# A hybrid decoder step: position bias as two more columns of the compression's products, and three reordered places

## The reference

```python
def nsa_compress(kv, w_ck1, w_ck2, w_cv1, w_cv2, pe_k, pe_v):     # CMP_STRIDE 16, CMP_BLK 32, CMP_HID 128
    ch = kv.reshape(B, n_chunks, 16, 2, NSA_KV_HEADS, HEAD_DIM)
    blocks = jnp.concatenate([ch[:, j:j + n_cmp] for j in range(2)], axis=2)
    def mlp(x, pe, w1, w2):
        x = (x + pe[None, None, :, None, :]).transpose(0, 3, 1, 2, 4).reshape(B, NSA_KV_HEADS, n_cmp, 32 * HEAD_DIM)
        return jax.nn.silu(x @ w1) @ w2
    kc = mlp(blocks[:, :, :, 0], pe_k, w_ck1, w_ck2)
    vc = mlp(blocks[:, :, :, 1], pe_v, w_cv1, w_cv2)

z = rmsnorm(x, g_attn_norm) @ w_in        # prompt 512 rows, samples 8 rows; q, k, v, compression k/v, gates
y = rmsnorm(x3, g_final)                  # x3: the residual after the MLP; y_prompt and y_sample
```

## Time and profile before

| what | us |
|---|---|
| launches: median of 3 (lowest, highest) | 1170.24 (1166.24, 1178.13) |
| the profiled execution's own time | 1176.75 |
| its span in the trace | 1174.9 |
| TensorE products busy | 1080.7 (92%) |
| VectorE, ScalarE, GpSimd busy | 620.0, 393.0, 61.7 |
| mean granted TensorE clock, as a share of full speed | 0.933 |

### The profile page before, as it was taken

One profiled execution on the slowest core, in us unless ns is written; L12 is line 12 of the kernel. 1 busy time (PEld: TensorE's weight loads), 2 busy tenths in 40 slices (PEclk: granted clock), 3 DMA queues, 4 the chain that ended last, 5 costly groups with the idle time before them and its releaser, 6 DMA issues.

```text
span 1174.9 us, 23099 instructions
## 1 busy us (share of the span) xinstructions
PE 1080.7 (92%) x8348; PEld 953.1 (81%) x8348; DVE 620.0 (53%) x1052; ACT 393.0 (33%) x729; POOL 61.7 (5%) x83
## 2 busy tenths in 40 slices
PE   5996999998999898889998988999999999998994
PEld 4995999887888886555555557999999999998994
DVE  4333663577778677676444446445543334553334
ACT  4220112333333334656445345322221112221223
POOL 1000001211111100000000000110000000000000
PEclk9997996798999987899999998999999999999998
DMA  8537229599999963165766671323333333333221
GB/s 301 171 115 150 79 87 238 155 262 242 256 263 274 254 209 125 62 202 183 238 195 206 207 226 37 90 72 89 89 108 90 89 90 89 90 89 90 85 78 73
DMA packets 180323, 177.61 MB, mean 151 GB/s; under 512 B 13127, under 2 KB 140868, under 8 KB 177892
## 3 DMA queue, kind: packets, MB, share of 16 engines
q1 hardware_dynamic: 178536, 169.72, 51.4%
q10 hardware_dynamic: 1724, 7.04, 1.8%
HBM read 170.83 MB, written 10.06 MB: 154 GB/s over the span
## 4 chain that ended last, share of the span: by engine, by line
PE 63%; SPq 18%; issue 6%; DVE 5%; DMA 4%; ACT 3%; ACTq 0%; DVEq 0%
PE bank L658 59%; SPq L572 4%; PE bank L662 4%; SPq L494 3%; SPq L536 2%; SPq L560 2%; SPq L539 2%; SPq L487 2%; DMA low_arena<-in_cache_nsa_slc_kv_dram 2%; DMA high_arena<-in_w_in_dram 1%; DMA page_ids<-in_page_table_dram 0%; DMA high_arena<-in_cache_sb_kv_dram 0%; SPq L578 0%; SPq L500 0%; DVE high_arena L2197 0%
## 5 line engine op out<-in xcount | busy, mean ns | idle before, releaser
L658 PE MATMUL bank<-high_arena 128*128 128x254 f32 (+8 forms) x1864 | 241.3, 345 | 17.0 <-DMA high_arena<-in_cache_sb_kv_dram 7.3
L658 PEld LDWEIGHTS bank<-high_arena 128*128 128x128 f32 (+5 forms) x1864 | 187.5, 153 | 53.8 <-issue 12.6
L2126 DVE TENSOR_TENSOR w_low<-high_arena,w_high 128x1024 fp32r<-128x1024 f32 x72 | 90.1, 1251 | 78.8 <-ACT w_high L1502 68.8
L662 PE MATMUL bank<-low_arena 128*128 128x128 f32 (+3 forms) x658 | 106.6, 307 | 23.4 <-DMA low_arena<-in_cache_nsa_slc_kv_dram 11.5
L1502 ACT ACTIVATE w_high<-high_arena 128x1024 fp32r<-128x1024 f32 x72 | 76.4, 1061 | 144.4 <-PE bank L658 144.4
L662 PEld LDWEIGHTS bank<-low_arena 128*128 128x128 f32 (+3 forms) x658 | 87.5, 163 | 33.6 <-DMA low_arena<-in_cache_nsa_slc_kv_dram 12.2
L658 PE MATMUL bank<-a_high,w_high 128*128 128x256 f32 (+1 forms) x512 | 103.6, 284 | 5.3 <-issue 2.9
L658 PE MATMUL bank<-h_high,w_high 128*128 128x256 f32 (+1 forms) x512 | 103.7, 284 | 1.8 <-DVE h_low L2153 1.8
L658 PE MATMUL bank<-h_high,w_low 128*128 128x256 f32 (+1 forms) x512 | 103.8, 284 | 0.0
L658 PE MATMUL bank<-h_low,w_high 128*128 128x256 f32 (+1 forms) x512 | 103.8, 284 | 0.0
L658 PE MATMUL bank<-a_low,w_high 128*128 128x256 f32 (+1 forms) x512 | 103.2, 283 | 0.0
(11 more groups left out here) (226 smaller groups left out, 1583.3 us busy)
## 6 DMA issues: line engine op xcount, KB each, us to landing
low_arena<-in_cache_sb_kv_dram SPq DMA_DIRECT2D x128, 256.0 KB, 5.3
high_arena<-in_cache_sb_kv_dram SPq DMA_DIRECT2D x128, 256.0 KB, 3.5
high_arena<-in_cache_nsa_cmp_kv_dram SPq DMA_DIRECT2D x128, 128.0 KB, 5.3
high_arena<-in_w_up_dram SPq DMA_DIRECT2D x32, 512.0 KB, 4.0
high_arena<-in_w_down_dram SPq DMA_DIRECT2D x32, 512.0 KB, 4.2
high_arena<-in_w_in_dram SPq DMA_DIRECT2D x10, 1136.0 KB, 5.6
low_arena<-in_cache_nsa_slc_kv_dram SPq DMA_DIRECT2D x128, 64.0 KB
high_arena<-in_cache_nsa_slc_kv_dram SPq DMA_DIRECT2D x128, 64.0 KB, 2.4
```

The source lines that it names most:

```text
L658: return T.matmul(out, lhsT=l, rhs=r, start=start, stop=stop, **k)
L662: return T.transpose(out, in_, ident[0:n, 0:n])
L2126: V.tensor_tensor(w_lo_r[u], w_raw[u], w_hi[u], ALU.subtract).then_inc(sem(f"w_lo{u}"), 1)
```

## The change

Four edits. (1) Position bias: DVE writes the embedding as two further columns (32 and 33) of `xT`, so that the prompt's products of 66 instead of 62 columns form the bias in the last column of each head; the 32 one-column products and the common wait go. DVE copies the bias out of the bank for keys and for values apart (`bias(kv)`), and ACT waits for it before the sigmoid's first step. (2) SP loads block 6 before the first 8 pages of sample 0, block 7 before the other 8, then blocks 8 and 9. (3) At the start PE takes the samples' and six blocks of tile 0 before `vrow`; DVE scales tile 1 before it copies `vcol`; ACT makes two of the copies of `h_high` before the second half of block 0 and the two loads. (4) POOL waits for the last residual sum (`x3`) before it multiplies the samples' rows.

```diff
@@ -157,8 +157,8 @@
 SIGNALS = {
-    "start_pe": ["vcol_mm", "pe_mm"],
-    "start_dve": ["st_set", "ss", "vcol_ev", "hs_in", "qscaled", "gates", "pebias", "pebias"],
+    "start_pe": ["vcol_mm"],
+    "start_dve": ["st_set", "ss", "vcol_ev", "hs_in", "qscaled", "pe_cols", "gates", "pebias", "pebias"],
     "start_act": ["rt"] * 5 + ["w_hi_first", "gates_e"],
@@ -472,15 +472,19 @@
                 if t == 0:
-                    sp.dma_start(ident, A["consts"][:, 0:P]).then_inc(sem("vrow_in"), 16)
+                    sp.dma_start(ident, A["consts"][:, 0:P]).then_inc(sem("x_in0"), 16)
             w_in_v = w_in.rearrange("(k p) c -> p k c", p=P)
+            def load_block(u, turn, col):
+                sp.wait_ge(sem(f"win_free{u}"), turn + 1)
+                sp.dma_start(win[u][:, :, :], w_in_v[:, :, ds(col, CB)]).then_inc(sem(f"win_in{u}"), 16)
...
                     for u in range(2):
-                        sp.wait_ge(sem(f"win_free{u}"), i + turn + 1)
-                        sp.dma_start(win[u][:, :, :], w_in_v[:, :, ds(i * (2 * CB) + (u * CB + col), CB)]).then_inc(sem(f"win_in{u}"), 16)
+                        load_block(u, i + turn, i * (2 * CB) + (u * CB + col))
@@ -500,11 +504,12 @@
                 sp.dma_start(w2[kv], A[n][0]).then_inc(sem("cmpw_in"), 16)
-            sp.wait_ge(sem("vrow_in"), 16 * 9)
+            sp.wait_ge(sem("vrow_in"), 16 * 8)
             sp.wait_ge(sem("hT_mm"), 9)
-            for half in range(2):
-                load_chunks(page_ids(8 * half), 0, half)
-            load_columns(*COLUMNS[1])
+            for u in range(2):
+                load_block(u, FIRST // 2, u * CB)
+                load_chunks(page_ids(8 * u), 0, u)
+            load_columns(FIRST // 2 + 1, (NCB - FIRST) // 2 - 1, 2 * CB)
@@ -661,22 +666,29 @@
-            pe.wait_ge(sem("vrow_in"), 16 * 9)
-            tr(bank[3][:, 0:56], vrow[0:56, :]).then_inc(sem("start_pe"), 1)
+            def rows_T(t, ks):
+                pe.wait_ge(sem("h_ready"), t + 2)
+                for k in ks:
+                    ins = tr(bank[k][:, t * P:(t + 1) * P], h[:, t, k * P:(k + 1) * P])
+                    if t == NT - 1:
+                        ins.then_inc(sem("hT_mm"), 1)
+            pe.wait_ge(sem("x_in0"), 32)
             pe.wait_ge(sem("h_ready"), 1)
...
             ins.then_inc(sem("hT_mm"), 1)
-            for t in range(NT):
-                pe.wait_ge(sem("h_ready"), t + 2)
-                for k in range(KD):
-                    if t == 0 and k == 3:
-                        pe.wait_ge(*signal("vcol_ev", 1))
-                    if t == 0 and k == 7:
-                        pe.wait_ge(*signal("hs_in", 1))
-                    ins = tr(bank[k][:, t * P:(t + 1) * P], h[:, t, k * P:(k + 1) * P])
-                    if t == NT - 1:
-                        ins.then_inc(sem("hT_mm"), 1)
+            rows_T(0, (0, 1, 2, 4, 5, 6))
+            pe.wait_ge(sem("vrow_in"), 16 * 8)
+            tr(bank[3][:, 0:56], vrow[0:56, :]).then_inc(sem("start_pe"), 1)
+            rows_T(1, (0, 1, 2, 4, 5, 6))
+            pe.wait_ge(*signal("vcol_ev", 1))
+            pe.wait_ge(*signal("hs_in", 1))
+            for t in range(2):
+                rows_T(t, (3, 7))
+            for t in range(2, NT):
+                rows_T(t, range(KD))
@@ -743,15 +755,10 @@
             pe.wait_ge(sem("cmpw_in"), 64)
-            for kv in range(2):
-                for m in range(16):
-                    ins = mm(bank[6][:, kv:kv + 1], w1[kv][:, m, :], vcol[:, 24 + 16 * kv + m:25 + 16 * kv + m],
-                             m == 0, m == 15)
-            ins.then_inc(sem("start_pe"), 1)
             for j in range(2):
...
             pe.wait_ge(sem("qkT_ev0"), 8)
-            pe.wait_ge(*signal("pebias", 2))
+            pe.wait_ge(*signal("pe_cols", 1))
@@ -775,6 +782,7 @@
                 nb = n - 1 if tiles == 2 else NCP
+                nh = nb if tiles == 2 else NCP + 2
                 past = int(tiles == 2)
@@ -796,10 +804,10 @@
                         pe.wait_ge(sem(f"xT_ev{half}"), c * 4 + (kv * 2 + qp + 4 * past * (1 - half)) + 1 + 1)
-                    out = bank[2 + kv][:, 0:KVH * nb].rearrange("p (h c) -> p h c", h=KVH)
+                    out = bank[2 + kv][:, 0:KVH * nh].rearrange("p (h c) -> p h c", h=KVH)
                     for m in (2 * qp, 2 * qp + 1, 2 * qp + 4, 2 * qp + 5):
-                        mm(out, w1[kv][:, m, :], xT[kv][:, m, :, 0:nb], m == 0, False)
-                        ins = mm(out, w1[kv][:, 8 + m, :], xT[kv][:, m, :, 1:nb + 1], False, m == 7)
+                        mm(out, w1[kv][:, m, :], xT[kv][:, m, :, 0:nh], m == 0, False)
+                        ins = mm(out, w1[kv][:, 8 + m, :], xT[kv][:, m, :, 1:nh + 1], False, m == 7)
                     if qp == 1:
@@ -1142,7 +1150,7 @@
             pe.wait_ge(sem("n_pT"), NSA_U)
-            pe.wait_ge(sem("x_in0"), 16 + 32)
+            pe.wait_ge(sem("x_in0"), 32 + 32)
             out_residual(0)
@@ -1227,7 +1235,7 @@
             for t in range(NT):
-                act.wait_ge(sem(f"x_in{t}"), 16)
+                act.wait_ge(sem(f"x_in{t}"), 16 if t else 32)
                 chain(S.activation(h[:, t, :], x[:, t, :], ACT.Square, accum_out=st[:, t:t + 1]))
@@ -1247,12 +1255,13 @@
             S.activation(win_hi_r[0][:, 0:KD // 2], win[0][:, 0:KD // 2], ACT.Copy).then_inc(sem("start_act"), 1)
-            S.activation(win_hi_r[0][:, KD // 2:], win[0][:, KD // 2:], ACT.Copy).then_inc(sem("w_hi0"), 1)
-            act.dma_start(win_first, A["w_in"][0].rearrange("(k p) c -> p k c", p=P)[:, :, (NCB - FIRST) * CB:(NCB - FIRST + 1) * CB]
-                          ).then_inc(sem("first_in"), 16)
-            act.dma_start(const[:, P:NCONST], A["consts"][:, P:NCONST]).then_inc(sem("const_in"), 16)
             act.wait_ge(*signal("vcol_ev", 1))
             for k in range(KD):
+                if k == 2:
+                    S.activation(win_hi_r[0][:, KD // 2:], win[0][:, KD // 2:], ACT.Copy).then_inc(sem("w_hi0"), 1)
+                    act.dma_start(win_first, A["w_in"][0].rearrange("(k p) c -> p k c", p=P)[:, :, (NCB - FIRST) * CB:(NCB - FIRST + 1) * CB]
+                                  ).then_inc(sem("first_in"), 16)
+                    act.dma_start(const[:, P:NCONST], A["consts"][:, P:NCONST]).then_inc(sem("const_in"), 16)
                 act.wait_ge(sem("hT_mm"), k + 1 + 1)
@@ -1302,8 +1311,6 @@
-            act.wait_ge(*signal("pebias", 2))
             def keys_out(i, u, q):
@@ -1327,8 +1335,10 @@
                     act.wait_ge(sem(f"hid_ready{kv}"), c + past + 1)
+                    if tiles == 1:
+                        act.wait_ge(*signal("pebias", kv + 1))
                     e = hid[kv][:, :, 0:nb]
-                    chain(S.activation(e, bank[2 + kv][:, 0:KVH * nb].rearrange("p (h c) -> p h c", h=KVH),
+                    chain(S.activation(e, bank[2 + kv][:, 0:KVH * nh].rearrange("p (h c) -> p h c", h=KVH)[:, :, 0:nb],
                                        ACT.Exp, bias=pebias[:, 2 + kv:3 + kv], scale=-1.0))
@@ -1619,14 +1629,15 @@
             row_scale(NT, 1)
-            row_scale(0, 2)
+            for t in range(2):
+                row_scale(t, t + 2)
             dve.wait_ge(*signal("vcol_mm", 1))
...
                             over(vcol[:, 0:KD], 2, B), ALU.mult).then_inc(sem("start_dve"), 1)
-            for t in range(1, NT):
+            for t in range(2, NT):
                 row_scale(t, t + 2)
@@ -1706,6 +1717,10 @@
             V.memset(st[0:1, 204:205], 0.0).then_inc(sem("start_dve"), 1)
+            for kv in range(2):
+                ins = V.tensor_copy(xT[kv][:, :, :, NCP + 1:NCP + 3],
+                                    over(vcol[:, 24 + 16 * kv:40 + 16 * kv].rearrange("p (two m) -> p m two", two=2), 2, KVH))
+            ins.then_inc(sem("start_dve"), 1)
             for j in range(0, 14, 2):
@@ -1737,11 +1752,13 @@
-            dve.wait_ge(*signal("pe_mm", 1))
-            V.tensor_copy(pebias[:, 0:2], bank[6][:, 0:2]).then_inc(sem("start_dve"), 1)
-            V.tensor_scalar(pebias[:, 2:4], bank[6][:, 0:2], -1.0, None, ALU.mult).then_inc(sem("start_dve"), 1)
-            dve.wait_ge(*signal("pebias", 2))
             dve.wait_ge(*signal("gates", 1))
+            def bias(kv):
+                dve.wait_ge(sem(f"hid_mm{kv}"), 1)
+                col = bank[2 + kv][:, NCP + 1:NCP + 2]
+                chain(V.tensor_copy(pebias[:, kv:kv + 1], col))
+                V.tensor_scalar(pebias[:, 2 + kv:3 + kv], col, -1.0, None, ALU.mult).then_inc(sem("start_dve"), 1)
@@ -1750,7 +1767,8 @@
                 dve.wait_ge(sem(f"w2_mm{kv}"), c + past + 1)
-                hp = bank[2 + kv][:, 0:KVH * nb].rearrange("p (h c) -> p h c", h=KVH)
+                nh = nb if past else NCP + 2
+                hp = bank[2 + kv][:, 0:KVH * nh].rearrange("p (h c) -> p h c", h=KVH)[:, :, 0:nb]
                 V.scalar_tensor_tensor(out=hid[2 + kv][:, :, 0:nb], in0=hp, scalar=pebias[:, kv:kv + 1], in1=e,
```

(6 more changed lines are left out.)

## The result

Median of 14 runs of the changed kernel: **1159.43 us** (1150.55 to 1169.88). The kernel before, on the same chips: 1172.16 us (14 runs, 1166.24 to 1178.13). The ratio is 0.989, 95% interval 0.9864 to 0.9915, a gain of 12.7 us by the medians and of 11.4 by the means (1172.2 and 1160.8), where 19.4 were forecast. The direction is right; the time lies 1.4 us above the range and 8.4 us above the forecast. Two of the 14 runs (1168.03 and 1169.88) count as slow, over 1.5% above the fastest one, and are left out of the ratio; without them the mean is 1159.4.

The account below looks back on a forecast made before the run. TensorE's products were busy in 92% of the span, so gains must remove products, PE's waits or time at the lower clock. 13.5 + 4.3 + 0.3 + 1.3 = 19.4 us off 1170.24 gave 1151, range 1144 to 1158.

Parts of the forecast that it names:

- Load order, 13.5 forecast: Projection: block 6 issued ahead of the pages removes PE's 11.1 us wait and 2.4 of slower products; bounds 11 and 13.9.
- rival (b): Projection: pages take the blocks' bandwidth; 1180 in full (chance 0.02), 1161 with one block late (0.06).
- No wait of PE for `w_in` and ten blocks of about 13.85: Sign expected in the profile after: projection blocks of about 13.85 us each, PE never waiting for their columns.
- Rival (d): Projection: load order does little in a median launch, the wait being long only in the profiled execution; 1157.5, chance 0.10.
- Bias, 4.3 forecast: Prompt's compression: 5.0 gained at ACT's first copy, less 0.2 for added columns and 0.5 for the values' half.
- I count it whole: Samples' loop: its transfer stream starts 4.3 us earlier with unchanged work, so the bias edit's gain passes through entirely.
- rival (a): Samples' loop: bound by its transfers, it takes back the bias edit's gain; 1155, chance 0.10.
- Start, 0.3 forecast: Start: PE's transposes end some 2 us sooner, row tile 0 of block 0 0.5 to 0.7; bounds -1.5 and +1.5.
- The worry: Start: the two loads, now behind two ACT copies, would be issued 0.8 us later and delay block 1's rounding.
- Last sum, 1.3 forecast: End: DVE's last residual sum takes 0.70 us instead of 2.03 with POOL's multiplication behind it; bounds 0.8 and 1.4.
- in which I see none of the four terms: Base of the forecast: the profiled execution's 6.5 us above the median held none of the gains, so all 19.4 applied to 1170.24.
- the forecast's own, 1146 to 1156: Whole launch: the range given for the forecast of 1151 us itself, before the rivals; the forecast's chance was 0.62.

Follow-up runs that it names:

- x_load: The kernel before with only the load order of the change; mean 1156.9 ± 1.8 us, ratio 0.9867.
- m_act: The changed kernel with ACT's six small transfers issued later, in its pause before the values' sigmoid of the prompt's compression; mean 1153.5 ± 1.2 us, ratio 0.9851.
- r_idle_mm: n_best with the 32 old one-column products put back at their place, their result unused; mean 1156.6 ± 0.9 us, ratio 0.9885.
- r_old_bias: n_best with the bias computed as before the change, by 32 one-column products; mean 1154.1 ± 0.8 us, ratio 0.9856.
- n_best: The changed kernel without the start edit, with SP waiting for landed columns before each set of pages and ACT's six small transfers later; mean 1148.3 ± 1.6 us.
- m_wait: The changed kernel with SP waiting until block 6 (block 7) has landed before issuing the eight pages behind it; mean 1157.3 ± 2.4 us, ratio 0.9872.
- x_load_act: x_load with ACT's six small transfers issued later, before the values' sigmoid, and the old bias products; mean 1160.2 ± 0.8 us, ratio 0.9902.

## Why the prediction was wrong

**Load order, 13.5 forecast, 12.1 ± 1.1 by the fit: right in mechanism and nearly in size.** The pages stood ahead of block 6's columns, and their going behind removes the wait. The 13.48 was one execution's, where five give 11.6; and the new order leaves 0.8 and 0.7 us in blocks 5 and 6 of this profile, 1.1 in the mean of seven traces, because pages behind a block delay it, which rival (b) had in a far larger form. "No wait of PE for `w_in` and ten blocks of about 13.85" is refuted by PE's waits of 0.8 and 0.6 us in these blocks. Rival (d), that the order does little in a median launch, is out: x_load alone gives 14.8 ± 1.9.

**Bias, 4.3 forecast: the step that failed is "I count it whole".** Everything up to the loop's start came as worked out: ACT's last issue sets the first chunk copy (5.0 forecast, 5.02 between the two profiles, 3.9 against the mean of the old ones, since the products take 9.4 to 12.2 us by when the clock falls), 66 columns cost nothing, the values' half 0.5. In the time 0.0 ± 1.0 is left, outside the term's bounds of 3.3 and 5 and as rival (a) had it, and that is half of what separates 1151 from 1159. Rival (a)'s mechanism, transfers that bind the loop, isn't shown: the loop lasts 236 us with the edit and 235 without in the mean of the traces (231 to 244), and m_act's 5.9 us and r_idle_mm's 9.3 pass through the same loop whole.

What takes back the 3.4 stays open. The traces could hide it: from the loop's start to the end they scatter by more than 3 us among kernels with the same work there. One reading is some 2 us of real gain, at the edge of the fit's interval. The other is a cost behind the stage in every kernel with the columns. The runs lean to it: if the shift at the loop's start is taken whole, all 218 are fitted as well (4.4 us) with 3.5 ± 0.8 us lost wherever the columns stand, and in the traces the time from the loop's start to the end is 959.7 us in the nine with them and 956.5 in the eight without, 3.3 ± 1.8 more; r_idle_mm's trace, at 952.2, doesn't fit in. PE's 6.2 us of idling ahead of the chunk transposes isn't this cost, since m_act removes the idling and the loss stays: the edits on bias and transfers together give 5.5 ± 1.6 where the loop starts 9.8 earlier. No run shows what the columns, which nothing reads after the prompt's compression, could cost there.

What the runs do show is that the edit was half of one: with ACT's transfers out of the way it is worth 5.8 ± 1.8 (r_old_bias against n_best).

**Start, 0.3 forecast, +1.8 ± 0.9 (a loss): the step that failed is the worth of PE's earlier transposes.** The worry had the wrong object. The loads were issued at 14.21, 0.1 later than before and not 0.8. PE's transposes end 3.1 us sooner (14.74, 17.81 before), but its first product comes only at 18.03 (18.47 before), 3.29 us later, when POOL has made the low part of block 0's first half. That runs from 15.29 to 17.88 now and from 15.34 to 17.94 before; the forecast left it out. Block 0 ends some 0.4 us sooner on average (37.35 in six traces, 37.78 in eleven). But block 1 has no lead of its own: it lasts 13.8 to 19.6 us by when block 2's columns land, 16.5 in the mean with the edit and 15.2 without, and an earlier end of block 0 doesn't bring these columns sooner (they land at 45.2 in the mean with the edit, 44.6 without). Why, no run shows. The 0.9 us between the means of block 1's end are no more than their own scatter, and the loss of 1.8 is two of its standard errors.

**Last sum, 1.3 forecast: shown at its place.** Line 2186 takes 0.70 us both times, as POOL's 2.07 begin only at its end; over the 18 traces the last sum takes 0.70 in the ten with the edit and 2.03 or 2.04 in the eight without. In the time the fit has 0.5 ± 0.9, within which 1.3 fits.

**The sum.** The fit gives 12.1 + 0.0 - 1.8 + 0.5 = 10.8 for the change, measured 11.4 ± 1.8 by the means. The forecast's 19.4 is 8.6 above the fit: 4.3 from the bias, 2.1 from the start, 1.4 from the load order and 0.8 from the last sum. By the medians it is 6.7 above the measured 12.7, and the base lay another 1.9 too low (1170.24 of three runs, against 1172.16). The remark that the profiled execution was 6.5 above the median "in which I see none of the four terms" was the second slip: 1.9 of the load term was in it. And the range that was called the forecast's own, 1146 to 1156, isn't the sum of the terms' bounds, which give 13.6 to 21.8 us, 1148 to 1157.

## What to carry to other kernels

When a step is removed from one engine and another engine's queue ends behind it only a few microseconds later, cost the two as one: here neither the bias products nor the moved transfers alone were worth anything that the runs could find, and together they gave 5.5 us (the fit), or 9.8 at the loop's start. Read a stall from several launches before you book it, and hold a transfer that must land against everything that is issued behind it; a wait in the queue until it has landed was worth its 1.1 us, and perhaps more (3.0 ± 1.3 by the fit). A term of under 2 us in a kernel whose launches scatter by 4.4 belongs in the range, not in the sum.

## What the runs showed of the hardware

- Eight pages (1 MB) issued 1.4 us behind a block of columns (128 x 2272 values of 4 bytes) on the same queue delay its landing from 5.6 to 6.8 us (the changed kernel's first set against m_wait; over 13 traces 5.9 to 6.9 us with the pages behind, 5.4 to 6.0 with the pages held back).
- TensorE's granted clock goes to 0.50 (the level of 1.2 GHz) at most 2.7 us behind the first chunk transposes of the prompt's compression, or before them, and stays there until the samples' loop has begun, in all 18 traces. It falls again at changing places later: one stretch of unchanged work took 263.3 to 274.8 us, the shortest at a mean clock of 0.91, the longest at 0.88.
- The same 64 one-column instructions take 9.37 us in r_old_bias, where the clock falls 4.9 us after their start, and 12.20 in x_load_act, where it falls 1.8 us after it.
- ACT's first use after six small transfer issues comes only at their end: 3.9 us of issuing (175.64 to 179.58) held a copy whose input was ready.
